# Layer 1's attention: turned weight groups in pairs, every other slot

## The reference

```python
def block(args):
    qi, i = args
    logits = jnp.einsum('bqhd,bkhd->bhqk', qi, kf) * scale
    mask = key_pos[None, :] < q_pos[:, None]
    log_keep = jnp.where(mask, jax.nn.log_sigmoid(-logits), 0.0)
    later = lax.cumsum(log_keep, axis=3, reverse=True) - log_keep
    weights = jnp.where(mask, jnp.exp(jax.nn.log_sigmoid(logits) + later), 0.0)
    return jnp.einsum('bhqk,bkhd->bqhd', weights, vf)
```

## Time and profile before

| | |
|---|---|
| runs, median (lowest to highest) | 2253.42 us (2251.48 to 2254.99) |
| the profiled execution: its span, first to last instruction | 2258.5 us |
| PE busy over the span | 2216.4 us, 98% |
| DVE, ACT, POOL busy | 1581.9, 914.2, 263.5 us |
| the attention's slots with the tail | about 60 to 431 us of the span |
| granted TensorE clock, mean | 0.990 of full speed |

### The profile page before, as it was taken

How to read it: one execution, slowest core, us unless ns; L and a number is a source line. 1 busy time by engine, 2 the same in 40 slices (tenths; PEclk the granted TensorE clock), 3 DMA queues, 4 the chain that set the end, 5 groups by cost and what they waited for, 6 DMA issues and landing times. The chain is left out here.

```text
span 2258.5 us, 34288 instructions
## 1 busy us (share of the span) xinstructions
PE 2216.4 (98%) x13052; PEld 1823.0 (81%) x13052; DVE 1581.9 (70%) x2212; ACT 914.2 (40%) x1672; POOL 263.5 (12%) x266
## 2 busy tenths in 40 slices
PE   8999999999999999999999989999999999999997
PEld 7888888888888887887877777887888888888886
DVE  5657678876665545657687788887798777765557
ACT  5443544343343321243344445555533333324444
POOL 0222232100000000001232222322020000000000
PEclk9999999999999999999999989999999999999999
DMA  4111111144333264433233442323235444448655
GB/s 152 47 38 58 37 56 38 66 147 157 116 114 111 86 261 175 150 111 122 85 112 112 150 141 72 107 93 112 96 131 191 163 158 163 158 156 299 214 181 184
DMA packets 106952, 289.06 MB, mean 128 GB/s; under 512 B 9692, under 2 KB 35388, under 8 KB 102332
## 3 DMA queue, kind: packets, MB, share of 16 engines
q1 hardware_dynamic: 106812, 287.14, 36.2%
HBM read 205.01 MB, written 82.10 MB: 127 GB/s over the span
## 5 line engine op out<-in xcount | busy, mean ns | idle before, releaser
L124 PE MATMUL psG<-h_hi,w_hi 128*128 128x512 f32 (+1 forms) x624 | 164.4, 395 | 2.1 <-DVE features_T L1875 1.6
L124 PE MATMUL psG<-h_hi,w_lo 128*128 128x512 f32 (+1 forms) x624 | 161.6, 391 | 0.0
L124 PE MATMUL psG<-h_lo,w_hi 128*128 128x512 f32 (+1 forms) x624 | 161.4, 392 | 0.0
L455 POOL TENSOR_TENSOR sb_w<-sb_left 128x128 f32<-128x128 f32 (+3 forms) x96 | 96.9, 1014 | 320.3 <-DVE sb_left L582 320.3
L124 PEld LDWEIGHTS psG<-h_hi,w_hi 128*128 128x128 f32 x624 | 109.9, 188 | 23.7 <-DVE features_T L1875 2.9
L124 PEld LDWEIGHTS psG<-h_hi,w_lo 128*128 128x128 f32 x624 | 111.4, 188 | 20.2 <-DVE w_lo L155 0.2
L124 PEld LDWEIGHTS psG<-h_lo,w_hi 128*128 128x128 f32 x624 | 111.1, 188 | 20.1 <-issue 0.5
L582 DVE TENSOR_TENSOR_SCAN sb_left<-sb_left 128x128 f32<-128x128 f32 (+3 forms) x96 | 102.7, 1078 | 2.1 <-ACT sb_left L468 1.4
L150 ACT CAST w_hi<-w_raw 128x1024 fp32r<-128x1024 f32 x48 | 50.3, 1049 | 120.0 <-PE psG L124 61.7
L155 DVE TENSOR_TENSOR w_lo<-w_raw,w_hi 128x1024 fp32r<-128x1024 f32 x48 | 58.6, 1222 | 55.0 <-ACT w_hi L150 55.0
L2024 POOL TENSOR_TENSOR features_T<-m_bias_both 128x512 f32<-128x512 f32 x10 | 16.8, 1675 | 680.3 <-DMA m_bias_both<-in_proj_pairs 633.0
(11 more groups left out here) (657 smaller groups left out, 5949.8 us busy)
## 6 DMA issues: line engine op xcount, KB each, us to landing
w_raw<-in_units SPq DMA_DIRECT2D x76, 512.0 KB, 4.3
w_raw<-hidden_blocks SPq DMA_DIRECT2D x77, 256.0 KB, 2.9
merge_gates<-features_T SPq DMA_DIRECT2D x12, 1024.0 KB, 6.7
merge_gates<-merge_gates SPq DMA_DIRECT2D x12, 1024.0 KB, 4.8
features<-features_T SPq DMA_DIRECT2D x24, 512.0 KB, 3.8
w_spare<-in_units SPq DMA_DIRECT2D x22, 512.0 KB, 4.4
down_sums<-w_spare SPq DMA_DIRECT2D x22, 512.0 KB, 3.3
hidden_blocks<-features_T SPq DMA_DIRECT2D x11, 1024.0 KB, 3.9
```

What stands on the lines that cost most here:

```text
L124: return pe.matmul(out, lhs, rhs, start=first, stop=last, skip_group_check=True)
L455: pool.tensor_tensor(w, left_chunk(S, 1), left_chunk(S), ALU.subtract).then_inc(w_ready, 1)
```

## The change

One table changes. In a half-round the slots in which the ten groups are turned become 7; 9, 9; 11; 13, 13; 15, 15; 17, 17 in place of 7; 8, 9; 11; 12, 13; 14, 15; 16, 17:

```diff
-BACK_SLOTS = ((7,), (8, 9), (11, 12, 13), (14, 15, 16, 17))
+BACK_SLOTS = ((7,), (9, 9), (11, 13, 13), (15, 15, 17, 17))
```

## The result

The changed kernel takes 2260.45 us (median of 8 runs, 2258.11 to 2265.91) beside 2253.64 us for the kernel before (8 runs, 2251.48 to 2259.12): a ratio of 1.0029, 95% interval 1.0019 to 1.0040, or 4 to 9 us more. The forecast was 2259.0 us, slower.

What follows compares the result with a forecast made beforehand. PE, busy 98% of the span, was taken as the bound, so added PE waits lengthen the run: 3.0 + 1.8 + 0.65 + 0.2 = 5.65 us, 5.6 taken, on 2253.4 gives 2259.0 us; own range 2257 to 2261, stated range 2254.5 to 2262.5.

Steps and rivals of the forecast that it cites:

- The turn that leaves the slot ahead of a `gate_add` wait: Slots 13, 25, 37, 49, 73, 85, 97: PE waits longer by the turn of four blocks that left, 7 x 0.43 = 3.0 us.
- The same, one pair earlier: Turns leaving slots 20, 32, 44, 80, 92 lengthen `gate_add` waits: 0.43 at slot 81 plus 4 x 0.34 = 1.4 us.
- The term of slot 81: PE already idles 0.53 us there for `gate_add`; the turn that leaves slot 80 adds 0.43 us.
- Slot 28 and 29: Slot 28 loses a turn and a `values`, 0.95 us; PE waits 0.65 us for its late sigmoid before slot 29's logits.
- In the other even slots ... the sigmoid was further ahead than what they lose: Other even slots following a projection unit's end: no sigmoid wait, or one merging with a `gate_add` wait already counted.
- the room is larger than the turn: The three remaining places of the earlier pair: room before `values` exceeds the turn (slot 69: 0.61 against 0.43), so nothing.
- odd slots: They get a second `values` and turn; copies on ACT and DVE, POOL's `difference` and SP's queue were costed at nothing.
- The tail: Last two groups turned together; the last low part waits for the other tile's copies: 0.2 us taken, between 0 and 0.69.
- the third rival: A pair's second tile comes late for `values` in the tail's three pairs: 3.9 us more, 2262.9; chance 0.08.
- A turn of eight at 0.86 us, no gain: Eight blocks in one visit cost 0.89 us against 0.86 for two visits of four; no gain or loss taken.
- The clock: Rival: eight transposes of a pair drop the granted clock to 1.2 GHz, 28 us more, 2287; chance 0.01.
- The marks: Signs if right: line 425 releasing psO's loads eleven or twelve times, PE busy time unchanged; if wrong: waits for line 590.

Runs made afterwards that it cites:

- Part 2 alone: Kernel before, with only the third pair p's groups moved, to slots (11, 13, 13) from (11, 12, 13): 2262.61 against 2254.02 us, ratio 1.0032.
- Part 1 alone: Kernel before, with only the second pair p's groups moved, to slots (9, 9) from (8, 9): 2255.15 against 2254.02 us, ratio 1.0007.
- the version with two visits: Changed kernel with the second turn of a slot one projection group later on PE: 2258.62 us against 2254.02 us for the kernel before, ratio 1.0024.
- the version without the waits: Kernel before with move_out and gate_add one slot earlier and the copy of k one slot later: 2244.82 against 2255.17 us, ratio 0.9962.

## Why the prediction was right, point by point

*The turn that leaves the slot ahead of a `gate_add` wait: right.* Seven times 0.43 was forecast, 3.0 us; the steps sum to 2.93. Part 2 alone shows six of them, and with psO moved out earlier they vanish.

*The same, one pair earlier: the mechanism right, the size too low.* The term of 4 x 0.34 measured 1.76 us with slot 91's. I had taken off 0.09 us of room in each. Part 1 alone gives .40 to .44, the whole turn: the 0.09 between `gate_add` and `values` in the earlier trace rows is not room. The weight load of that `values` shows it: before, it has already waited 0.21 us and stands 0.07 us behind the end of `gate_add` (137.91), with the matmul behind it at 138.05; after, `gate_add` ends at 139.01, the load stands 0.07 behind it and the matmul at 139.11. Before, then after:

```profile
137.98 0.19 PEld L124 LDWEIGHTS psO<-sb_w_lo,sb_v_both 128*128 128x128 f32 x1 [0.21 <-issue]
```

```profile
139.08 0.19 PEld L124 LDWEIGHTS psO<-sb_w_lo,sb_v_both 128*128 128x128 f32 x1 [0.45 <-issue]
```

The term of slot 81, 0.43, measured 0.40, but at another place: V's turn in slot 78 waits first, for ACT's evacuation. Slot 81's own wait is 0.47 us, against 0.53 before; in part 1 alone, where slot 78 keeps its `values`, it is 0.97 us, as the prediction says.

```profile
358.48 0.98 PE L758 MATMUL psG<-c_ident,features_T 128*128 128x128 f32 x7 [0.29 <-ACT pool_v L524]
...
367.82 0.36 PE L124 MATMUL psO<-sb_w_lo,sb_v_both 128*128 128x256 f32 x1 [0.47 <-issue]
```

*Slot 28 and 29: right.* 0.65 was forecast, 0.73 measured, again with a weight load in the open; the copies of k moved away take it off.

*"In the other even slots ... the sigmoid was further ahead than what they lose": failed at slot 75.* Slot 74 loses 0.95 us, as slot 28 does, and the two high parts of slot 73 push the copies of q and the sigmoid of slot 74 back on ACT, so that 0.26 us show. I had looked at the room on PE's side and not at what the pair adds on ACT ahead of it.

The same sentence has slots 78 and 90 wrong: V's turn, which it does not name, and the sigmoid of slot 90 had less room than the `values` that left. There the rest of the sentence holds, the wait merges with a `gate_add` wait that was counted.

*Slot 61: "the room is larger than the turn", and odd slots, "I cost them at nothing", failed.* Slot 60 too loses its turn of four blocks (0.43 us). `gate_add` ended at 293.27 before and `values` started at 294.02, so 0.70 us of room seemed enough. But the room shrank. In slot 57 the pair's two low parts stand ahead of `split_lo` (line 155) on DVE. SP's load of the next weights (line 145) waits for that, the store of the attention (line 417) stands behind this load in SP's queue, and the `gate_add` of slot 60 waits until the store has landed, 5.5 us after its issue before and 5.7 us after. Before, then after:

```profile
285.40 1.22 DVE L155 TENSOR_TENSOR w_lo<-w_raw,w_hi 128x1024 fp32r<-128x1024 f32 x1
...
286.65 0.33 SPq L145 DMA_DIRECT2D w_raw<-in_units  x1
...
287.02 0.43 SPq L417 DMA_DIRECT2D y_branches<-features_T  x1
...
292.59 0.68 DVE L425 TENSOR_TENSOR features_T<-psO,sb_o_sum 64x512 f32<-64x512 f32 x1 [0.55 <-DMA y_branches<-features_T]
```

```profile
287.01 1.16 DVE L590 TENSOR_TENSOR sb_w_lo<-psT,sb_w_hi 128x512 fp32r<-128x512 f32 x2 [2.47 <-ACT sb_w_hi L476]
...
290.06 1.22 DVE L155 TENSOR_TENSOR w_lo<-w_raw,w_hi 128x1024 fp32r<-128x1024 f32 x1
...
291.31 0.33 SPq L145 DMA_DIRECT2D w_raw<-in_units  x1
...
291.68 0.43 SPq L417 DMA_DIRECT2D y_branches<-features_T  x1
...
297.45 0.68 DVE L425 TENSOR_TENSOR features_T<-psO,sb_o_sum 64x512 f32<-64x512 f32 x1 [0.76 <-DMA y_branches<-features_T]
```

Line 155 comes 4.66 us later where PE's slots are only some 4.3 us later; the store and `gate_add` follow by 4.66 and 4.86. I had written that SP's queue does not change. Its order doesn't; its times do. Against the end of ACT's split (283.95 before, 288.31 after) line 155 is 0.30 us late. Neither part does it alone: part 1 has the pair in slot 57, with the same 0.30, and no step at 61, since slot 60 keeps its turn; part 2 has the missing turn without the pair, and +.27. The store took 5.4 to 5.8 us to land in these four runs, so some of the step may be this one execution's. That the store holds `gate_add` is read from the releaser in the rows; the runs with psO moved out earlier issue the store earlier too and have no step here, but none moved the store alone.

*The tail: 0.2 taken, 0.25 measured, by luck.* The term meant the last pair, whose low parts would hold up DVE's sums for the merge. Those sums (line 1128) start 0.15 us later against the last `values`, and the merge's first product comes 0.15 us earlier all the same. The 0.25 us stand elsewhere: the first low part of slot 97's pair, behind line 155, comes too late for its `values`. That is the third rival, the late tile, in one place of the three where it was priced at 1.3 us at most.

*A turn of eight at 0.86 us, no gain: right,* by the version with two visits. The clock stayed at 1.00 over 32 runs of seven or eight transposes. The Trainium skill (TensorE: Matmul & The Clock Gate, section "Part 4: PE-mode transpose") says that transposes do not count as activity for the clock in the way that matmuls do; no run here shows a fall.

*The marks.* Line 425 was named as the releaser eight times and not eleven or twelve: in the other places the same wait stands under "issue" or first as a wait for the sigmoid in the same slot. PE's busy time was to stay unchanged and rose by 2.1 us; the last section says why. I had also called a wait for line 590 a mark of error; there is one, the tail's, and it is one: a late tile, not the tail's term.

What was too low (0.4 for four places, 0.1 at slot 29, 0.7 at 61 and 75) and what was not foreseen on the other side (the small savings, 0.5, and the merge) nearly cancel: 5.65 forecast, 6.0 measured. So the mechanism of the large terms was right, and that the total came so close is luck.

## What to carry to other kernels

When PE is 98% busy and an accumulator is emptied on a chain that PE does not drive, what matters of a moved PE step is on which side of that wait it ends up; the fullest gain is to start the chain earlier. When work is grouped, follow it on the other engines too: a second tile on ACT or DVE delays everything that stands behind it in that queue, including a store that SP issues and a later step that waits for its DMA. Read the room in front of a wait from the weight load and not from its matmul: a seeming room of 0.09 us was none here.

## What the runs showed of the hardware

*A busy PE includes part of its waits.* Before, 351.03 us of the stretch are busy, after 353.16, and 348.87 in the version without the waits, all for the same matmuls. A matmul that has waited is longer in the record (0.39 us for the waited `values` of slot 13, 0.28 to 0.29 for those behind it), and in a run of matmuls the modelled end of one lies under the next, which a wait uncovers. So the record shows 4.0 us of idle time in the stretch before, while the stretch without the waits is 5.9 us shorter (355.00 against 349.06).

*DVE and POOL seem to block each other.* In the tail after:

```profile
423.31 1.26 DVE L648 SCALAR_TENSOR_TENSOR features_T<-pool_v,features_T 128x1024 f32<-128x1024 f32 x1
...
423.47 1.99 POOL L455 TENSOR_TENSOR sb_w<-sb_left 128x512 f32<-128x512 f32 x1 [6.09 <-DVE sb_left L582]
...
424.49 2.06 DVE L155 TENSOR_TENSOR w_lo<-w_raw,w_hi 128x1024 fp32r<-128x1024 f32 x1
...
426.57 1.16 DVE L590 TENSOR_TENSOR sb_w_lo<-psT,sb_w_hi 128x512 fp32r<-128x512 f32 x2
427.32 0.19 PEld L124 LDWEIGHTS psO<-sb_w_lo,sb_v_both 128*128 128x128 f32 x1 [0.45 <-DVE sb_w_lo L590]
```

The same `difference` took 1.04 us in the tail before, and line 155 takes 1.23 us elsewhere. The rows fit, to some 0.15 us, a turn-taking: `difference` starts 0.16 us behind line 648 and runs its 1.04 us only once that has ended (424.57), and line 155, at 424.49, runs its 1.23 us once `difference` has ended (425.46). The Trainium skill (SBUF — State Buffer, section "Who interferes with whom") says that a DVE instruction with two SBUF inputs contends with a GpSimd instruction that reads SBUF, and that the port pair which they share is an exclusive lock. These rows agree; no run here was made to test it. POOL's busy time in the stretch, 94.53 us before, 103.12 after and 84.97 in the best version, is longer with the waits for the same work, as such meetings would make it. The one that showed on PE lies in the tail: the pair's low parts stand behind line 155, and the first of them, done at 427.27, releases a weight load at 427.32 that has waited for 0.45 us.
